# Layer norms of a two-block transformer kernel: centred on the mean of the first half of the tiles, with their sums inside the product ahead

## The chip, the cores and the metric

The kernel runs on one core of a Trainium2 chip. The time is device microseconds from the first to the last instruction's work of one launch; lower is better. Engines are named as in the profile: PE is TensorE (PEld its weight loads), DVE VectorE, ACT ScalarE, SP the queue that issues the DMAs.

## What is computed

Two blocks of two layers each on 256 tokens of width 2048, all in float32. The change concerns the first block:

```python
for layer in range(2):
    y = mixer(x) @ w_out                          # layer 0: rwkv7 + rglru, layer 1: sparse attention
    x = layer_norm(ALPHA * x + y, ln1_g, ln1_b)
    x = layer_norm(ALPHA * x + conv_ffn(x), ln2_g, ln2_b)
    x = x + sigmoid(x @ ple_w_gate) * (p[layer] @ ple_w_proj)

def layer_norm(x, g, b, eps=1e-5):
    mu = mean(x); var = mean((x - mu) ** 2)
    return (x - mu) * rsqrt(var + eps) * g + b
```

The second block (RMS norms, three attentions, gates) follows and is not changed.

## The kernel before

**Layout.** Activations lie as 16 tiles of 128 features by 256 tokens (`xav`, `xbv`), so that a mean over features is a sum over partitions and tiles: a matmul with a 128x128 matrix of ones (`m("ones")`), one per tile, gives it, repeated on all partitions. `res` is the buffer that takes ALPHA * x + y, `x` the input; after the norm `x` holds the result.

**A product.** Weights come in pieces of 2 MB (1.4 MB for `down`) into a ring of three slots. Each piece has two halves of 128 output features. ACT rounds a half to fp32r (`split`, high part, semaphore `w_hi`), DVE subtracts to get the low part (`w_lo`), and PE does three groups of matmuls: high weights on the high and on the low part of the activations, low weights on the high part. There is one buffer per half, so ACT can write it only when PE has done with it. A unit is two halves into one PSUM bank, or, for the `up` products, into a bank per half; three banks take turns (`bank_free`), five more take the small jobs (`open_job`, `done`). A `down` unit has four pieces. The activations are split in the same way, in four parts of four tiles (`rhs`; `r_hi` from ACT, `r_lo` from DVE).

**A norm.** There are four: `ln0` after `ev_out`, `ln1` after `down0`, `ln2` after `od_out`, `ln3` after `down1`. `residual` evicts each unit on DVE. When all are out, `layer_norm` runs on three engines: PE sums 16 tiles (L783), DVE centres them (L1881) and ACT squares them (L1440), PE sums the squares (L802), then variance, square root, reciprocal, and for each part scaling on DVE, gain and bias on two tiles by each engine, and the split. The next product, `up` or `pg`, takes high parts first, then low parts. After `ln1` and `ln3` PE also does the embedding product `pp` (eight units of four f32 matmuls, L767), which DVE evicts behind the norm (L2386).

**Order.** Every engine's order is the order of the code. Products with many units are hardware loops over three units (`rounds`, L342) where no `after` function is given: `ev_out`, `od_out`, `down0`, `down1`, `pg0` and the `up` products among them.

**The first mixer's input product** `ea`, `eb`, `ec` goes by weight halves p = 0 to 42, with the mixer's element work beside them, keyed to p on each engine. At p = 29 PE sums the squares of `kk` (L852), at p = 33 it spreads their reciprocal roots (L861); at p = 42 DVE makes `KM`, on which the semaphore `elem` stands.

## Time and profile before

| | |
|---|---|
| median of 3 runs | 3715.66 us (3715.22 to 3721.29) |
| profiled execution, its own time | 3714.28 us |
| its span | 3712.5 us |
| PE busy | 3494.2 us (94%) |
| DVE busy | 2196.9 us (59%) |
| ACT busy | 1691.6 us (46%) |
| DMA, mean over the span | 152 GB/s |
| mean granted clock of PE | 0.970 |

The granted clock is a share of 2.4 GHz; the other level is 1.2 GHz, 0.50. In a timeline row the first two numbers are the start and the length in us, and the bracket at its end is the idle time of the engine ahead of it and who ended it; f32 matmuls have two records per instruction.

### The profile page before, as it was taken

What the parts mean: (1) busy time and instruction counts of PE and PEld (TensorE: products, weight loads), DVE (VectorE), ACT (ScalarE), POOL (GpSimd) and SP (SyncE); (2) the same over time, 40 slices, a digit from 0 to 9 for tenths busy, and PEclk for the clock granted to TensorE, in tenths of its full rate; (3) what the DMA queues carried; (4) which work ended last, traced back from release to release, by engine and by line L of the source; (5) the groups of instructions that cost most, each with busy time, mean ns of one, the idle gap of its engine ahead of it and who ended that gap; (6) DMA issues with size and microseconds to landing.
All of it is one profiled execution on the core that took longest, in us unless ns stands there. A gap on an engine that the chain in (4) does not pass through costs nothing.

```text
span 3712.5 us, 56634 instructions
## 1 busy us (share of the span) xinstructions
PE 3494.2 (94%) x23204; PEld 3196.2 (86%) x23204; DVE 2196.9 (59%) x2674; ACT 1691.6 (46%) x2030; POOL 0.2 (0%) x4
## 2 busy tenths in 40 slices
PE   8988969999998998988989999989989999899988
PEld 7878969788888997977988888889989888898878
DVE  5485764666666345535456666654456568456674
ACT  4562223565556333423345566553344455344553
POOL 0000000000000000000000000000000000000000
PEclk9999979999999999999999999999999999999999
DMA  6440025355553443531334454444524434444332
GB/s 254 159 159 24 2 91 181 127 190 181 186 198 131 165 181 134 188 150 55 123 126 182 183 195 187 167 152 177 209 114 172 173 134 148 157 150 183 135 140 110
DMA packets 45084, 563.78 MB, mean 152 GB/s; under 512 B 4832, under 2 KB 7024, under 8 KB 8048
## 3 DMA queue, kind: packets, MB, share of 16 engines
q1 hardware_dynamic: 44912, 561.27, 40.9%
q8 instruction: 134, 2.20, 0.2%
q14 instruction: 38, 0.31, 0.0%
HBM read 559.13 MB, written 2.12 MB: 151 GB/s over the span
## 4 chain that ended last, share of the span: by engine, by line
PE 85%; DVE 7%; ACT 4%; issue 3%; DMA 1%; DVEq 0%; ACTq 0%; SPq 0%
PE bank L707 28%; PE bank L711 15%; PE bank L657 5%; PE bank L653 5%; PE bank L648 5%; PE bank L748 4%; PE bank L751 4%; PE bank L756 4%; PE bank L783 4%; PE bank L767 2%; DVE ring L1875 1%; ACT spl_r L1365 1%; DVE scr L1881 1%; PE bank L802 1%; PE bank L954 1%
## 5 line engine op out<-in xcount | busy, mean ns | idle before, releaser
L1875 DVE TENSOR_TENSOR spl_r<-ring,spl_r 128x2048 fp32r<-128x2048 f32 x415 | 950.1, 2291 | 657.5 <-ACT spl_r L1365 656.2
L707 PE MATMUL bank<-all_r,spl_r 128*128 128x512 f32 x5008 | 1212.2, 394 | 1.6 <-ACT spl_r L1365 1.6
L1365 ACT ACTIVATE spl_r<-ring 128x2048 fp32r<-128x2048 f32 x415 | 793.1, 1912 | 759.9 <-PE bank L711 400.4
L707 PEld LDWEIGHTS bank<-all_r,spl_r 128*128 128x128 f32 x5008 | 924.7, 189 | 192.3 <-issue 7.9
L711 PEld LDWEIGHTS bank<-all_r,spl_r 128*128 128x128 f32 x5104 | 654.6, 191 | 24.4
L711 PE MATMUL bank<-all_r,spl_r 128*128 128x256 f32 x5104 | 662.4, 283 | 0.0
L1875 DVE TENSOR_TENSOR dsp_r<-ring,dsp_r 128x1408 fp32r<-128x1408 f32 x128 | 207.3, 1625 | 290.4 <-ACT dsp_r L1365 290.4
L1365 ACT ACTIVATE dsp_r<-ring 128x1408 fp32r<-128x1408 f32 x128 | 175.6, 1377 | 297.3 <-PE bank L756 297.2
L1881 DVE SCALAR_TENSOR_TENSOR scr<-sumbuf,vec,scr 128x255 f32<-128x255 f32 (+1 forms) x379 | 183.0, 483 | 118.0 <-ACT scr L1458 80.7
L648 PE MATMUL bank<-scr_r,spl_r 128*128 128x256 f32 x1536 | 209.6, 290 | 37.6 <-ACT scr_r L1319 35.8
L648 PEld LDWEIGHTS bank<-scr_r,spl_r 128*128 128x128 f32 x1536 | 196.2, 195 | 41.3 <-ACT scr_r L1319 33.5
L748 PE MATMUL bank<-scr_r,dsp_r 128*128 128x256 f32 x1408 | 195.3, 288 | 26.6 <-ACT dsp_r L1365 22.2
L748 PEld LDWEIGHTS bank<-scr_r,dsp_r 128*128 128x128 f32 x1408 | 182.2, 196 | 27.3 <-ACT dsp_r L1365 23.8
L653 PE MATMUL bank<-scr_r,spl_r 128*128 128x256 f32 x1536 | 204.2, 287 | 0.0
L657 PE MATMUL bank<-scr_r,spl_r 128*128 128x256 f32 x1536 | 201.1, 284 | 1.3 <-DVE spl_r L1875 1.3
L653 PEld LDWEIGHTS bank<-scr_r,spl_r 128*128 128x128 f32 x1536 | 195.7, 196 | 0.0
L657 PEld LDWEIGHTS bank<-scr_r,spl_r 128*128 128x128 f32 x1536 | 192.3, 193 | 1.8 <-DVE spl_r L1875 1.8
L751 PE MATMUL bank<-lo_r,dsp_r 128*128 128x256 f32 x1408 | 193.3, 286 | 0.0
L756 PE MATMUL bank<-scr_r,dsp_r 128*128 128x256 f32 x1408 | 190.8, 284 | 0.0
L1458 ACT ACTIVATE scr<-sumbuf,vec 128x256 f32<-128x256 f32 x176 | 105.3, 598 | 187.6 <-DVE sumbuf L1875 187.4
L751 PEld LDWEIGHTS bank<-lo_r,dsp_r 128*128 128x128 f32 x1408 | 182.0, 196 | 1.2 <-issue 1.2
L756 PEld LDWEIGHTS bank<-scr_r,dsp_r 128*128 128x128 f32 x1408 | 179.2, 193 | 0.0
(335 smaller groups left out, 2972.3 us busy)
## 6 DMA issues: line engine op xcount, KB each, us to landing
ring<-in_up SPq DMA_DIRECT2D x88, 2048.0 KB, 8.0
ring<-in_down SPq DMA_DIRECT2D x64, 1408.0 KB, 6.0
ring<-in_ib SPq DMA_DIRECT2D x34, 2048.0 KB, 8.2
ring<-in_pg SPq DMA_DIRECT2D x16, 2048.0 KB, 8.1
ring<-in_out SPq DMA_DIRECT2D x16, 2048.0 KB, 7.8
ring<-in_in SPq DMA_DIRECT2D x12, 2048.0 KB, 7.9
ring<-in_ec SPq DMA_DIRECT2D x11, 2048.0 KB, 9.1
ring<-in_ea SPq DMA_DIRECT2D x9, 2048.0 KB, 8.3
```

What stands on the lines that cost most here:

```text
L648: mm(out_, WHI[half][:, kk, :], rhi[:, kk, :], start=i_ == 0, stop=False)
L653: mm(out_, WHI[half][:, kk, :], rlo[:, kk, :], start=False, stop=False)
L657: one = mm(out_, WLO[half][:, kk, :], rhi[:, kk, :], start=False, stop=kk == DT - 1)
L707: mm(b[:, :], WHI[half][:, kk, :], pair(name, kk), start=kk == 0, stop=False, skip_group_check=True)
L711: one = mm(main, WLO[half][:, kk, :], rhi[:, kk, :], start=False, stop=kk == DT - 1, skip_group_check=True)
L748: mm(out_, DHI[half][:, kk, :], HHI[:, piece * FC + kk, :], start=first and kk == 0, stop=False, skip_group_check=True)
L751: mm(out_, DHI[half][:, kk, :], HLO[:, low_slot(piece * FC + kk), :], start=False, stop=False, skip_group_check=True)
L756: one = mm(out_, DLO[half][:, kk, :], HHI[:, piece * FC + kk, :], start=False, stop=last and kk == FC - 1, skip_group_check=True)
L783: one = mm(out, lhsT, rhs, start=n == 0, stop=n == len(terms) - 1)
L1365: A(high[half], w[:, :, half * P:(half + 1) * P], ACT.Copy).then_inc(S["w_hi"], count)
L1875: return V.tensor_tensor(out, a, b, op)
L1881: return V.scalar_tensor_tensor(out=out, in0=a, scalar=s, in1=b, op0=op0, op1=op1)
```

## The change

`residual` and `layer_norm` become one function per engine, `normed` (DVE, ACT) and `norm_sums` (PE), called after every unit of the product, which is written out unit by unit.

- While units 1 to 3 come out, DVE adds the first eight tiles up pairwise into two tiles of `x`; behind unit 4 PE sums these two, and DVE subtracts this mean of the first half (`SV`) from the ten tiles that are out. Units 5 to 7 are centred on it in their eviction (`x` is scaled and lowered ahead of it).
- ACT squares as tiles come; DVE adds squares up to four tiles. PE sums tiles 8 to 15 (whose mean gives what is still missing) and the squares, 4 matmuls behind unit 6 and 10 behind unit 7.
- Behind that: variance as mean of squares less the square of the mean, square root with the bias eps on ACT, reciprocal, and per part recentring and scaling on DVE, gain and bias on all four tiles and the high part on ACT.
- The next product's unit 0 (`both_halves`) takes the activations part by part, for both weight halves.
- The embedding product's unit 0 goes ahead of the last sums, its other units behind them, and ACT evicts them. Its input is loaded behind the `up` weights, into another place.
- In the first mixer the `kk` sum goes from p = 29 to 30, the spreading from 33 to 35, and `KM` behind the loop over p.

```diff
@@ SP
             def embedding(l):
-                sp.wait_ge(S["g_done"], STEP0[f"pp{l}"])
+                sp.wait_ge(S["g_done"], STEP0[f"up{l}"] + 2)
                 sp.dma_start(PIN, dram["p"][l]).then_inc(S["in_p"], 16)
...
                 stream(f"up{l}", FT)
+                embedding(l)
                 stream(f"down{l}", 32)
                 load(f"pp{l}", 0)
-                stream(f"pg{l}", 8, (2, lambda: embedding(l)))
+                stream(f"pg{l}", 8)
@@ PE
+            def both_halves(name, high, low, units):
...
+                def from_high(part):
+                    pe.wait_ge(S["r_hi"], 4 * n + part + 1)
+                    for half, w in ((0, WHI[0]), (0, WLO[0]), (1, WHI[1])):
+                        for kk in range(4 * part, 4 * part + 4):
+                            fresh = kk == 0 and w is not WLO[0] and (half == 0 or len(units) == 2)
+                            mm(high[half], w[:, kk, :], rhi[:, kk, :], start=fresh, stop=False, skip_group_check=True)
...
+                from_high(0)
+                from_high(1)
+                from_high(2)
+                from_low(0)
+                from_high(3)
+                for part in range(1, 4):
+                    from_low(part)
+                pe.wait_ge(S["w_lo"], first + 2)
+                for kk in range(DT):
+                    one = mm(high[1], WLO[1][:, kk, :], rhi[:, kk, :], start=False, stop=kk == DT - 1,
+                             skip_group_check=True)
+                one.then_inc(S["g_done"], 1)
...
-                rounds(pe, UNITS[name][0], unit)
+                for k in range(UNITS[name][0]):
+                    unit(k, 0)
+                    after(k)
...
+            def norm_sums(n, name, x, res, k):
+                mean, var = (f"ln{n}_mean", 0), (f"ln{n}_var", 0)
+                if k == 4:
+                    b = open_job(mean)
+                    pe.wait_ge(S["ln_sum"], n + 1)
+                    done(acc(b[:, 0:T], [(m("ones"), x[:, i, :]) for i in range(2)]))
+                if k == 6:
+                    b = open_job(var)
+                    pe.wait_ge(S["ln_cent"], 3 * n + 3)
+                    pe.wait_ge(*free_of(name, 5))
+                    for i in range(8, 12):
+                        mm(b[:, T:2 * T], m("ones"), res[:, i, :], start=i == 8, stop=False, skip_group_check=True)
+                if k == 7:
+                    b = job_bank(JOB[var])
+                    pe.wait_ge(S["ln_add"], n + 1)
+                    for i in range(4):
+                        mm(b[:, 0:T], m("ones"), x[:, i, :], start=False, stop=False, skip_group_check=True)
+                    pe.wait_ge(*free_of(name, 6))
+                    for i in range(12, 16):
+                        if i == 14:
+                            pe.wait_ge(*free_of(name, 7))
+                        mm(b[:, T:2 * T], m("ones"), res[:, i, :], start=False, stop=i == 15, skip_group_check=True)
+                    pe.wait_ge(S["ln_sq"], 6 * n + 6)
+                    for i in range(14, 16):
+                        one = mm(b[:, 0:T], m("ones"), x[:, i, :], start=False, stop=i == 15, skip_group_check=True)
+                    done(one)
...
+                def after(k):
+                    if k == 7:
+                        pe.wait_ge(S["in_p"], 16 * (l + 1))
+                        arrived(f"pp{l}")
+                        embedded(0)
+                    norm_sums(2 * l + 1, f"down{l}", x, res, k)
+
+                down(f"down{l}", after)
+                for k in range(1, 8):
+                    embedded(k)
...
-                if p == 29:
+                if p == 30:
...
-                if p == 33:
+                if p == 35:
@@ ACT, def normed(name, n, x, res)
+                for k in range(8):
+                    if k < 7:
+                        ahead(k, 0)
+                    if k == 5:
+                        for part in range(3):
+                            act.wait_ge(S["ln_cent"], 3 * n + part + 1)
+                            square(4 * part, min(4 * part + 4, 10))
+                    if k >= 6:
+                        act.wait_ge(*free_of(name, k - 1))
+                        square(2 * k - 2, 2 * k)
+                    if k < 7:
+                        ahead(k, 1)
+                    elif not down_:
+                        split(nxt, 0, 0, 1, (0,))
+                act.wait_ge(*free_of(name, 7))
+                square(14, 16)
+                if down_:
+                    embedded(0)
+                act.wait_ge(S["ln_var"], n + 1)
+                A(RV, RV, ACT.Sqrt, bias=v("eps")).then_inc(S["ln_std"], 1)
+                if down_:
+                    embedded(1)
+                    split(nxt, 0, 0, 1, (0,))
+                    embedded(2)
+                    split(nxt, 0, 0, 1, (1,))
+                    embedded(3)
+                else:
+                    split(nxt, 0, 0, 1, (1,))
                 for part in range(4):
...
+                    high(part)
+                    if down_:
+                        embedded(4 + part)
@@ DVE, def normed(name, n, x, res)
+                def evict(k):
+                    u = UNIT0[name] + k
+                    pair_ = slice(2 * k, 2 * k + 2)
+                    if k > 4:
+                        link(stt(x[:, pair_, :], x[:, pair_, :], ALPHA, repeat(SV, 2), ALU.mult, ALU.subtract))
+                    unit_wait(name, k, 0)
...
+                for k in range(8):
+                    if k < 7:
+                        ahead(k, 0)
+                    else:
+                        ve.wait_ge(S["ln_sq"], 6 * n + 5)
+                        linked(add_squares(12, 2), S["ln_add"], n + 1)
+                        if not down_:
+                            split(nxt, 0, 0, 1, (0,))
+                    evict(k)
...
+                    if k == 4:
+                        key = (f"ln{n}_mean", 0)
+                        b = job_wait(key)
+                        linked(ts(SV, b[:, 0:T], 2.0 / D), job_free(JOB[key]), freed(JOB[key]))
+                        ve.wait_ge(*free_of(name, 4))
+                        for first, last in ((0, 4), (4, 8), (8, 10)):
+                            tt(res[:, first:last, :], res[:, first:last, :], repeat(SV, last - first), ALU.subtract)\
+                                .then_inc(S["ln_cent"], 1)
...
+                    if k < 7:
+                        ahead(k, 1)
...
+                cent(0)
+                ve.wait_ge(S["ln_std"], n + 1)
+                link(V.reciprocal(RV, RV))
+                scaled(0)
+                for part in range(1, 4):
+                    if down_ and part > 1:
+                        split(nxt, 0, 0, 1, (part - 2,))
+                    cent(part)
+                    scaled(part)
+                    if not down_ and part > 1:
+                        rhs(nxt, part - 2, part - 1)
...
-                if p == 42:
-                    tt(KM, ZK, CUM, ALU.mult).then_inc(S["elem"], 1)
+            tt(KM, ZK, CUM, ALU.mult).then_inc(S["elem"], 1)
```

**TensorE at the end of `ev_out` and the start of `up0`, before.** `bank` is a PSUM bank, `xa` and `xb` the activation buffers, `mat` holds the ones.

```order
L653 MATMUL bank<-scr_r,spl_r 128x256 x16
L657 MATMUL bank<-scr_r,spl_r 128x256 x16
L783 MATMUL bank<-xb,mat 128x256 x16
L802 MATMUL bank<-xa,mat 128x256 x16
L698 MATMUL bank<-all_r,spl_r 128x256 x16
L703 MATMUL bank<-all_r,spl_r 128x256 x16
L711 MATMUL bank<-all_r,spl_r 128x256 x16
L707 MATMUL bank<-all_r,spl_r 128x512 x16
L711 MATMUL bank<-all_r,spl_r 128x256 x16
```

The same place after the change:

```order
L662 MATMUL bank<-scr_r,spl_r 128x256 x16
L666 MATMUL bank<-scr_r,spl_r 128x256 x16
L868 MATMUL bank<-xa,mat 128x256 x4
L873 MATMUL bank<-xb,mat 128x256 x4
L876 MATMUL bank<-xa,mat 128x256 x2
L742 MATMUL bank<-all_r,spl_r 128x256 x36
L748 MATMUL bank<-all_r,spl_r 128x256 x8
L742 MATMUL bank<-all_r,spl_r 128x256 x12
L748 MATMUL bank<-all_r,spl_r 128x256 x24
L762 MATMUL bank<-all_r,spl_r 128x256 x16
```

The 32 matmuls on ones behind the last product matmul are now ten (six more stand in the product, two behind unit 4, four behind unit 6), and unit 0 of `up0` comes in groups by part.

**ScalarE from the last `down0` weights to the high parts for `pg0`, before.** `dsp_r` and `spl_r` are rounded weights, `scr_r` the high part of the activations, `rstd` and later `xtra` the row of variances.

```order
L1365 ACTIVATE dsp_r<-ring 128x1408 x8
L1365 ACTIVATE spl_r<-ring 128x2048 x2
L1440 ACTIVATE xa<-xb 128x1024 x4
L1443 ACT_TABLE_LOAD
L1443 ACTIVATE rstd<-rstd 128x256
L1314 ACTIVATE xa<-xa,vec 128x256 x2
L1319 ACTIVATE scr_r<-xa 128x1024
L1314 ACTIVATE xa<-xa,vec 128x256 x2
L1319 ACTIVATE scr_r<-xa 128x1024
L1314 ACTIVATE xa<-xa,vec 128x256 x2
```

The same place after the change:

```order
L1435 ACTIVATE dsp_r<-ring 128x1408 x6
L1513 ACTIVATE xa<-xb 128x512 x2
L1518 ACTIVATE scr<-bank 128x512
L1549 ACT_TABLE_LOAD
L1549 ACTIVATE xtra<-xtra,vec 128x256
L1518 ACTIVATE scr<-bank 128x512
L1435 ACTIVATE spl_r<-ring 128x2048
L1518 ACTIVATE scr<-bank 128x512
L1435 ACTIVATE spl_r<-ring 128x2048
L1518 ACTIVATE scr<-bank 128x512
L1524 ACTIVATE xa<-xa,vec 128x256 x4
L1528 ACTIVATE scr_r<-xa 128x1024
```

The weight halves of `pg0` moved behind the square root, between copies of embedding units out of PSUM, of which three stand ahead of the first part and one behind each part; gain and bias go over four tiles instead of two.

**VectorE in the product `ev_out`, before,** in the last turn outside the loop:

```order
L1881 SCALAR_TENSOR_TENSOR xb<-xa,bank 128x512
L342 REGISTER_ALU
L342 COMPARE_AND_BRANCH
L1875 TENSOR_TENSOR spl_r<-ring,spl_r 128x2048 x2
L1881 SCALAR_TENSOR_TENSOR xb<-xa,bank 128x512 x2
```

After the change, around unit 4:

```order
L1986 TENSOR_TENSOR spl_r<-ring,spl_r 128x2048 x2
L1992 SCALAR_TENSOR_TENSOR xb<-xa,bank 128x512
L1989 TENSOR_SCALAR xtra<-bank 128x256
L1986 TENSOR_TENSOR xb<-xb,xtra 128x1024 x2
L1986 TENSOR_TENSOR xb<-xb,xtra 128x512
L1986 TENSOR_TENSOR spl_r<-ring,spl_r 128x2048 x2
L1992 SCALAR_TENSOR_TENSOR xa<-xa,xtra 128x512
L1986 TENSOR_TENSOR xb<-xa,bank 128x512
```

The mean of the first half and three centrings stand between the eviction of unit 4 and the low part of the next weight half.

## Rows read from the trace of the kernel before

**Rows 1.** The page's part 4: share of the chain that ended last, by engine.
```profile
PE 85%; DVE 7%; ACT 4%; issue 3%; DMA 1%; DVEq 0%; ACTq 0%; SPq 0%
```

**Rows 2.** Windows: start:end, length, busy us of each engine, granted clock, DMA share, GB/s.
```profile
634.00:677.00 43.00, 30.46 (x146) 26.43 (x145) 26.71 (x27) 18.40 (x21) 0.00 (x0) 0.84 0.14 50
1436.00:1491.00 55.00, 41.27 (x224) 36.86 (x225) 31.51 (x34) 19.68 (x21) 0.00 (x0) 0.91 0.23 91
1894.00:1938.00 44.00, 31.45 (x148) 26.92 (x148) 26.71 (x27) 19.58 (x22) 0.00 (x0) 0.81 0.13 48
2689.00:2744.00 55.00, 41.42 (x226) 37.01 (x227) 31.36 (x34) 19.54 (x21) 0.00 (x0) 0.91 0.23 91
```

**Rows 3.** Timeline of PE, first norm: start, us, engine, line, operation [idle before].
```profile
630.29 2.08 PE L653 MATMUL bank<-scr_r,spl_r 128*128 128x256 f32 x16
632.21 2.08 PE L657 MATMUL bank<-scr_r,spl_r 128*128 128x256 f32 x16
...
644.96 7.15 PE L802 MATMUL bank<-xa,mat 128*128 128x256 f32 x32 [2.50 <-ACT xa L1440]
658.49 1.19 PE L698 MATMUL bank<-all_r,spl_r 128*128 128x256 f32 x4 [6.38 <-ACT all_r L1319]
...
665.81 3.62 PE L703 MATMUL bank<-all_r,spl_r 128*128 128x256 f32 x16
...
675.29 2.08 PE L711 MATMUL bank<-all_r,spl_r 128*128 128x256 f32 x16
```

**Rows 4.** Timeline of PE, norm after down0, to unit 1 of pg0.
```profile
1434.28 1.48 PE L756 MATMUL bank<-scr_r,dsp_r 128*128 128x256 f32 x11
...
1453.42 5.34 PE L767 MATMUL bank<-scr,ring 128*128 128x256 f32 x24
...
1491.07 2.08 PE L648 MATMUL bank<-scr_r,spl_r 128*128 128x256 f32 x16
```

**Rows 5.** Timeline of DVE, end of ev_out and first norm.
```profile
613.24 2.29 DVE L1875 TENSOR_TENSOR spl_r<-ring,spl_r 128x2048 fp32r<-128x2048 f32 x1 [3.47 <-ACT spl_r L1365]
...
634.40 0.69 DVE L1881 SCALAR_TENSOR_TENSOR xb<-xa,bank 128x512 f32<-128x512 f32 x1 [6.75 <-PE bank L657]
...
653.05 1.75 DVE L2343 RECIPROCAL rstd<-rstd 128x256 f32<-128x256 f32 x1 [0.48 <-ACT rstd L1443]
654.84 1.23 DVE L1875 TENSOR_TENSOR xa<-xb,rstd 128x1024 f32<-128x1024 f32 x1
```

**Rows 6.** Timeline of ACT, first norm and up0; last row: pg0's first gate.
```profile
656.10 1.09 ACT L1314 ACTIVATE xa<-xa,vec 128x256 f32<-128x256 f32 x2 [3.08 <-DVE xa L1875]
657.28 1.06 ACT L1319 ACTIVATE all_r<-xa 128x1024 fp32r<-128x1024 f32 x1
...
671.84 1.91 ACT L1365 ACTIVATE spl_r<-ring 128x2048 fp32r<-128x2048 f32 x1 [5.80 <-PE bank L711]
...
1494.49 0.60 ACT L1481 ACTIVATE scr<-bank 128x512 f32<-128x512 f32 x1
```

**Rows 7.** Window in the first norm, columns as in the windows above.
```profile
662.00:666.00 4.00, 2.43 (x9) 2.14 (x10) 4.00 (x6) 3.89 (x5) 0.00 (x0) 0.50 0.00 0
```

**Rows 8.** Timeline of PE in the first mixer's input product and behind it.
```profile
209.80 1.94 PE L852 MATMUL bank<-scr,mat 128*32 128x256 f32 x16 [4.52 <-ACT scr L1581]
...
239.96 2.11 PE L861 MATMUL bank<-sumbuf,mat 32*128 32x256 f32 x16 [5.14 <-DVE sumbuf L2084]
...
297.27 2.73 PE L869 MATMUL bank<-mat,scr 128*128 128x128 f32 x16 [4.10 <-DVE scr L1881]
```

**Rows 9.** Window over the second half of the product ec.
```profile
211.58:297.21 85.63, 76.45 (x436) 66.44 (x432) 78.20 (x72) 45.47 (x61) 0.00 (x0) 0.95 0.31 111
```

**Rows 10.** Timeline of PE at the turn of down0's loop.
```profile
1273.39 1.61 PE L748 MATMUL bank<-scr_r,dsp_r 128*128 128x256 f32 x10 [3.23 <-issue]
1276.16 0.37 PE L748 MATMUL bank<-scr_r,dsp_r 128*128 128x256 f32 x1 [1.16 <-issue]
```

**Rows 11.** Window over the eight written-out units of pg1.
```profile
2744.00:2833.00 89.00, 88.16 (x714) 87.21 (x713) 48.70 (x44) 42.55 (x47) 0.00 (x0) 1.00 0.45 166
```

More of the change, by code:

```diff
@@ L509, in build, with free_of @@
             n_low += 2 * UNITS[name][0]
+        LN_NEXT = ("up0", "pg0", "up1", "pg1")
+        def free_of(name, k):
+            u = UNIT0[name] + k
+            return bank_free[u % R3], 2 * (u // R3) + 4
         def freed_unit(name, k, half, i):
@@ L1067, in _ @@
             group_norm_var(1)
-            product("ev_out")
-            layer_norm(0, xbv)
+            product("ev_out", after=lambda k: norm_sums(0, "ev_out", xav, xbv, k))
             ffn(0, xav, xbv)
@@ L1684, in _ @@
             rhs("ev_out", 2)
[L1685 to L1687 removed]
+            normed("ev_out", 0, xav, xbv)
             ffn(0, xav)
@@ L2324, in residual @@
-                for un in range(UNIT0[name] + 5, UNIT0[name] + 8):
-                    ve.wait_ge(bank_free[un % R3], 2 * (un // R3) + 4)
-                ve.engine_nop().then_inc(S["resid"] if scale != 1.0 else S["x_ready"],
-                                                            8 if scale != 1.0 else 1)
-            def layer_norm(n, res, dst, gain, bias, col):
-                split(("up0", "pg0", "up1", "pg1")[n], 0, 0)
-                b = job_wait((f"ln{n}_mean", 0))
-                for part in range(4):
-                    sl = slice(4 * part, 4 * part + 4)
-                    stt(res[:, sl, :], repeat(b[:, 0:T], 4), -1.0 / D, res[:, sl, :]).then_inc(S["ln_cent"], 1)
-                ve.wait_ge(S["ln_cent"], 4 * n + 4)
-                ve.engine_nop().then_inc(job_free(JOB[(f"ln{n}_mean", 0)]), 1)
+                else:
+                    rhs(name)
+                    split(name, 0, 0)
@@ L2343, in layer_norm @@
-                link(V.reciprocal(rstd[:, 0:T], rstd[:, 0:T]))
-                for part in range(4):
-                    sl = slice(4 * part, 4 * part + 4)
-                    linked(tt(dst[:, sl, :], res[:, sl, :], repeat(rstd[:, 0:T], 4), ALU.mult),
-                           S["ln_y"], 4 * n + part + 1)
-                    for i in range(4 * part, 4 * part + 2):
-                        one = ts(dst[:, i, :], dst[:, i, :], v(gain, col + i), v(bias, col + i), ALU.mult, ALU.add)
-                    one.then_inc(S["x_part"], 1)
@@ L2353, in layer_norm, with cent, scaled @@
-                rhs(("up0", "pg0", "up1", "pg1")[n])
+                def cent(part):
+                    sl = slice(4 * part, 4 * part + 4)
+                    link(tt(res[:, sl, :], res[:, sl, :], repeat(SV, 4), ALU.subtract))
+                def scaled(part):
+                    sl = slice(4 * part, 4 * part + 4)
+                    tt(x[:, sl, :], res[:, sl, :], repeat(RV, 4), ALU.mult).then_inc(S["ln_y"], 1)
+                cent(0)
+                ve.wait_ge(S["ln_std"], n + 1)
+                link(V.reciprocal(RV, RV))
```

190 lines of the change are left out of this document (107 added, 83 removed).

## The prediction

> **What bounds the kernel now.** I read the chain that ended last first: TensorE has 85% of it [rows 1], so time is won only where TensorE waits, or works on something that can go. The windows over the four layer norms come next [rows 2]. In the two after `ev_out` and `od_out` TensorE is busy for 30.46 of 43 us and 31.45 of 44 us; in the two after the `down` products for 41.27 and 41.42 of 55 us, and much of that is the sums of the norm and the embedding product. The reader is to see that a norm costs TensorE far more than its idle time, so I measure each norm from the last product matmul (T) to the end of the next product's unit 0.
>
> After `ev_out`, T is 632.21 + 2.08 = 634.3 us; the sums of squares end at 652.1, the first `up0` matmul starts at 658.49, and unit 0 ends when the pair of rows from 675.29 ends, at 677.2 [rows 3]: **42.9 us**. After `od_out` the same rows repeat (two norms of this kind) and the window is one us longer; by the same two matmuls it is **43.6 us**. After `down0` T is 1435.8, the embedding product starts at 1453.42 and unit 1 of `pg0` starts at 1491.07 [rows 4]: **55.3 us**. After `down1` the window [rows 2] has the same length and busy time; I take 55.2.
>
> **What the new sequence takes behind T.** Prices: a `ones` matmul on one f32 tile takes 7.15/16 = 0.45 us [rows 3], an embedding unit of four such tiles 5.34/3 = 1.8 [rows 4]. A product matmul takes, in steady pace 0.12 us (groups of 16 start 1.92 apart), and 3.62/16 = 0.226 at the low clock [rows 3]. VectorE: eviction of a unit 0.69, reciprocal 1.75, four tiles by a repeated row 1.23, low half of a weight half 2.29 [rows 5]. ScalarE: two gained tiles 1.09, copy of four tiles 1.06, high half of a weight half 1.91, a unit out of PSUM 0.60 [rows 6].
>
> After `ev_out`/`od_out`, in us behind T: the last eviction (0.8) and the last two squares on ScalarE (a pair of tiles, 0.60 by the nearest row [rows 6], to 1.5) lie beside ten `ones` matmuls, 10 x 0.45 = 4.5. Three small VectorE steps are not in this form in the trace; they are half as wide as an eviction (0.69), so between 0.35 and 0.7 each; with handing on I take 1.7 in all: 6.2. Recentring part 0 (1.23), reciprocal (1.75), scaling (1.23): 10.5. ScalarE's square root and its high half of weight half 1 lie beside these. Now ScalarE sets the pace: four gained tiles and a copy, 2 x 1.09 + 1.06 = 3.2 per part, where VectorE needs 2 x 1.23. Parts are ready at 13.8, 17.0, 20.2 and 23.4. TensorE works on each as it comes; behind the last stand 12 matmuls, 24 on low parts and 16 on the low weights of half 1, 52 x 0.12 = 6.2, and I add 2 for the clock and for the third part, on which 20 matmuls stand: **31.6**.
>
> The clock was at 0.50 from 662 to 666 us [rows 7], the lower level of 1.2 GHz, behind a pause of six us and short bursts. It was back before 675.29, where 16 matmuls take 2.08, and what came before that was unbroken matmuls from 665.81 on [rows 3]. After the change TensorE pauses about 9 us, and its bursts (12 matmuls, 2.7 us at that level, in every 3.2) are nearly unbroken, and quite so from part 2 on. So I let the clock be low for parts 0 to 2 and full for what stands behind part 3; if it came back only behind unit 0, the 52 matmuls would take 11.8 us instead of 6.2, rival (a).
>
> In-product costs: two `ones` matmuls behind unit 4 and four behind unit 6 go into TensorE's row, 6 x 0.45 = **2.7** per norm. VectorE gets up to 5.2 us more in unit 4 (0.69, a wait for the mean of 2 x 0.45, its copy of 0.4, three centrings of ten tiles, 3.1) between the two weight halves. Its low half then ends 7.5 us behind the unit's end, and TensorE wants it at 5.76 + 3.84 = 9.6: two us to spare, so nothing. In units 5 and 6 it is 0.69 + 0.69 + 1.23. VectorE works 5.3 of every 11.5 us there now (two of 2.29 and one of 0.69 [rows 5]); were that cover gone, up to 3 us per unit would show. In the `down` products a unit lasts 31.7 us and nothing shows.
>
> Gain there: 42.9 - 31.6 - 2.7 = 8.6 and 43.6 - 34.3 = 9.3.
>
> After the `down` products: an embedding unit (1.8) goes ahead of the ten `ones` matmuls: 6.3, row work to 8.0, square root 8.4. ScalarE then has three units out of PSUM (0.60) and two weight halves (1.91): 5.6, so 14.0 (at 8.4 + 5.6); this, not VectorE's scaling at 12.3, is last. Four parts of 3.2 with three copies of 0.60 between them: 14.0 + 12.9 + 1.8 = 28.7. The embedding's last unit waits for the PSUM bank that ScalarE empties behind part 0, about 17.9, and ends at 19.7; TensorE starts on parts 0 and 1 then and has done them when part 2 comes. Behind part 3: 6.2, plus 1.3 for pauses: **36.2**, with 2.7 in the product 38.9. Gain 16.4 and 16.3. That ScalarE empties the embedding's banks while TensorE has nothing else is most of this.
>
> Sum over the norms: 50.6.
>
> **The first mixer.** The sum for `kk` goes one weight half later, the product that spreads it two halves later. TensorE waited 4.52 and 5.14 us before them and then 4.10 before the transposes [rows 8]. These waits are not all to be had, for VectorE becomes last: from 211.58 to 297.21 us it is busy 78.20 of 85.63 us [rows 9], idle 7.4, and it can't begin earlier: its first step there is the low half of the next weights behind ScalarE's high half, and that stands behind the squares of `kk` which the first of the three waits names [rows 8]. `KM` (eight tiles, 2.3 by the row for four [rows 5]) goes behind the last shift, off the transposes' path. Upper bound 7.4 + 2.3 = 9.7, lower 3: following VectorE's steps with its splits I get 3.0 at once, some 2 of the small waits, and 2.3 from `KM`: **7.4**, near the upper row.
>
> **Loops written out.** `ev_out`, `od_out`, `down0`, `down1` and `pg0` were loops on three engines. In `down0` TensorE waited 3.23 + 1.16 us for "issue" at the turn of the loop [rows 10], and 33 matmuls behind it ran low, about 2.3 us more: **6.7**. `down1` shows no such gap, so between 0 (it comes at some other place) and 7.5; written-out stretches show none, as `pg1` with TensorE busy 88.16 of 89 us [rows 11]. I take 6.7, what `down0` shows. The Trainium skill (Runtime: NRT & Kernel Launch, "Instruction fetch mechanics") says that a taken branch whose target lies outside the part held in instruction memory stalls for a fetch, while straight code is fetched ahead. By it both `down` loops, with 1584 matmul and weight-load instructions in a turn, would have paid, 13.4 in all; the trace has one gap, 6.7.
>
> The embedding's input goes earlier in the SP queue, ahead of `down`'s weights; 0.26 MB among 2 MB loads, hidden behind the ring's three slots: 0.
>
> **Sum.** 50.6 + 7.4 + 6.7 = 64.7, less 2 for handings between engines that I have not counted = 62.7. From the profiled execution's 3714.28: 3651.6; it lies 1.4 under the median shown. I say **3652**.
>
> **Rivals.**
> (a) Low clock through unit 0 at each norm: 5 us more each, 3672. For it: the pause is longer than now. Against: TensorE is then busy 2.7 of every 3.2 us. 0.10.
> (b) The written-out code keeps the gap elsewhere and the first mixer gives only 3: 3652 + 6.7 + 4.4 = 3663. For it: `down1` had none without the change. 0.15.
> (c) VectorE's centring makes the weights' low halves late in units 4 to 6: up to 5 us a norm, 3672. Against: two us to spare by the sum. 0.10.
> (d) Slower: the written-out `down` units each bring a fetch gap like the one at the loop's turn. At 6.7 each, over 9 such gaps eat the gain; one in each of 16 `down` units gives 3652 + 107 = 3759. Against: the written-out stretch that shows none [rows 11]. 0.03.
> (e) The norms' tails are as long as now because ScalarE's doubled share (3.2 against 2.15 per part) eats what the sums gave: it costs 4.3 per norm, already in; no change overall needs four times that. 0.03.
> Forecast: 0.59.
>
> **The numbers.** The forecast's own bounds: row steps, clock and mixer, 3640 to 3662. To leave out 2 in 10 the range reaches into (a) and (c): 3638 to 3674. A difference under 0.2% (7.4 us) can't be told from none. Faster 0.94, same 0.03, slower 0.03.
>
> **What would show it.** Per norm: T to the end of unit 0 near 32 and 36 us; part 0 about 14 behind T after `ev_out`; embedding units evicted by ScalarE; no TensorE wait in units 4 to 7; TensorE's waits at the two `kk` matmuls gone and small waits for VectorE's low halves in their place; no issue gap in `down0`. Wrong would be the sum if ScalarE's parts came slower than 3.2 us, or the ten `ones` matmuls waited for squares.

## The result and the profile after

| | before | after |
|---|---|---|
| median | 3716.29 us (3715.22 to 3721.29, 4 runs) | 3634.31 us (3632.09 to 3638.96, 4 runs) |
| profiled execution, its span | 3714.28, 3712.5 us | 3633.78, 3632.0 us |
| granted clock, mean | 0.970 | 0.976 |

The ratio is 0.9778 with a 95% interval of 0.9762 to 0.9795: 82 us faster by the medians, 80.5 us by the profiled executions. I had forecast 3652 (3638 to 3674), 62.7 us. The sign was right; the gain was underestimated by 17.8 us (80.5 less 62.7), and the median lies 3.7 us below the range.

The page of the changed kernel: the first line of part 1, and part 4 by engine, against [rows 1]:

```profile
PE 3452.0 (95%) x23108; PEld 3161.6 (87%) x23108; DVE 2221.1 (61%) x2686; ACT 1715.1 (47%) x2086; POOL 0.2 (0%) x4
...
PE 84%; DVE 7%; ACT 5%; issue 3%; DMA 1%; DVEq 0%; ACTq 0%; SPq 0%
```

TensorE has 42 us less busy time than before (3494.2) in a span 80.5 us shorter. ScalarE has one point more of the chain, the work it took over in the norms.

The windows over the four tails, each from T to the first matmul behind unit 0, against [rows 2]; columns as there:

```profile
624.45:653.37 28.92, 19.22 (x118) 17.66 (x117) 20.23 (x19) 18.60 (x26) 0.00 (x0) 0.82 0.19 73
1407.35:1440.59 33.24, 30.61 (x183) 27.41 (x182) 22.37 (x20) 24.01 (x34) 0.00 (x0) 1.00 0.37 150
1849.17:1878.11 28.94, 18.06 (x119) 16.52 (x118) 20.25 (x19) 19.90 (x27) 0.00 (x0) 0.88 0.20 72
2632.09:2665.33 33.24, 30.61 (x182) 27.41 (x181) 22.37 (x20) 24.02 (x34) 0.00 (x0) 1.00 0.38 152
```

A tail is the time from T, the end of the last product matmul, to the end of the next product's unit 0. The tails were 42.9, 55.3, 43.6 and 55.2 us. They are now 28.9, 33.2, 28.9 and 33.2. Behind the `down` products TensorE is busy 30.61 of 33.24 us, where it was 41.27 of 55: the embedding product now fills the wait.

**The first norm.** TensorE (the timeline, as in [rows 3]):

```profile
624.45 1.89 PE L868 MATMUL bank<-xa,mat 128*128 128x256 f32 x8
...
627.90 1.03 PE L876 MATMUL bank<-xa,mat 128*128 128x256 f32 x4
637.96 5.82 PE L742 MATMUL bank<-all_r,spl_r 128*128 128x256 f32 x24 [9.03 <-ACT all_r L1528]
643.98 1.70 PE L742 MATMUL bank<-all_r,spl_r 128*128 128x256 f32 x12 [0.20 <-ACT all_r L1528]
...
647.04 1.70 PE L742 MATMUL bank<-all_r,spl_r 128*128 128x256 f32 x12 [0.40 <-ACT all_r L1528]
...
651.45 2.08 PE L762 MATMUL bank<-all_r,spl_r 128*128 128x256 f32 x16
653.37 2.00 PE L720 MATMUL bank<-all_r,spl_r 128*128 128x512 f32 x8
```

VectorE's row work and first part, and ScalarE's parts, in the same stretch:

```profile
630.35 1.22 DVE L1986 TENSOR_TENSOR xb<-xb,xtra 128x1024 f32<-128x1024 f32 x1
...
633.39 1.22 DVE L1986 TENSOR_TENSOR xa<-xb,xtra 128x1024 f32<-128x1024 f32 x1
```

```profile
634.65 2.08 ACT L1524 ACTIVATE xa<-xa,vec 128x256 f32<-128x256 f32 x4 [2.00 <-DVE xa L1986]
636.76 1.06 ACT L1528 ACTIVATE all_r<-xa 128x1024 fp32r<-128x1024 f32 x1
637.72 2.06 ACT L1524 ACTIVATE xa<-xa,vec 128x256 f32<-128x256 f32 x4
```

Read from T = 624.45, the sums are done at 4.5 us, the variance at 5.9, the first scaled part at 10.2 and part 0 at 13.5. Before, the sums ended 17.8 us behind T and the first `up0` matmul began at 24.2 [rows 3]. A part then comes every 3.06 us (634.65 to 637.72 on ScalarE), so part 3 is there at 22.6 (647.04). What stands behind it ends at 28.9, which is 6.3 us for 52 matmuls at 0.12. The records of neighbouring rows overlap, so a part's pace is read from starts, not from the sum of lengths.

**The second norm**, TensorE, against [rows 4]:

```profile
1407.35 1.89 PE L825 MATMUL bank<-xtra,ring 128*128 128x256 f32 x8
...
1424.12 1.99 PE L825 MATMUL bank<-xtra,ring 128*128 128x256 f32 x8 [0.21 <-ACT scr L1518]
1427.66 4.76 PE L742 MATMUL bank<-scr_r,spl_r 128*128 128x256 f32 x36 [1.54 <-ACT scr L1518]
...
1434.26 1.69 PE L742 MATMUL bank<-scr_r,spl_r 128*128 128x256 f32 x12 [0.88 <-ACT scr_r L1528]
```

and before, the embedding's other units, whose wait [rows 4] does not show:

```profile
1469.23 10.50 PE L767 MATMUL bank<-scr,ring 128*128 128x256 f32 x40 [10.47 <-DVE scr L2386]
```

ScalarE empties the embedding's banks (`scr`, L1518), and TensorE waits 0.21, 1.54 and 0.88 us in the whole tail. Before, it waited 1.00 and 2.50 us at the sums, and 10.47 us for VectorE's eviction behind the embedding's third unit.

**The first mixer**, TensorE's waits, against [rows 8]:

```profile
207.16 1.07 PE L934 MATMUL bank<-scr,mat 128*32 128x256 f32 x16
...
238.10 2.17 PE L724 MATMUL bank<-all_r,spl_r 128*128 128x256 f32 x16 [2.37 <-DVE spl_r L1986]
240.20 1.17 PE L943 MATMUL bank<-sumbuf,mat 32*128 32x256 f32 x16
...
285.40 3.49 PE L951 MATMUL bank<-mat,scr 128*128 128x128 f32 x16 [4.34 <-DVE scr L1992]
```

The two waits at the `kk` matmuls (4.52 and 5.14 us) are gone. In their place stand three for VectorE's low halves, 1.08, 2.37 and 0.25 us. The wait before the transposes is still there, 4.34 us where it was 4.10: `KM` is out of VectorE's way, but TensorE arrives earlier. No wait of TensorE for "issue" is left in `down0`, nor one for anything in the units 4 to 7 of `ev_out`.

### The profile page after: what moved, and what is told of

Same layout as the page of the kernel before. It is cut to its first block, busy times and chain, and to the rows that moved or that the text cites. A ratio compares the mean times of both kernels' runs of the same rounds, so it can differ in the third digit from the quotient of the medians.

```text
span 3632.0 us, 56135 instructions
## 1 busy us (share of the span) xinstructions
PE 3452.0 (95%) x23108; PEld 3161.6 (87%) x23108; DVE 2221.1 (61%) x2686; ACT 1715.1 (47%) x2086; POOL 0.2 (0%) x4
## 3 DMA queue, kind: packets, MB, share of 16 engines
q8 instruction: 144, 2.36, 0.3%
## 4 chain that ended last, share of the span: by engine, by line
PE 84%; DVE 7%; ACT 5%; issue 3%; DMA 1%; DVEq 0%; ACTq 0%; SPq 0%
PE bank L720 28%; PE bank L724 15%; PE bank L666 5%; PE bank L662 5%; PE bank L657 5%; PE bank L804 4%; PE bank L807 4%; PE bank L812 4%; PE bank L841 3%; PE bank L825 2%; ACT spl_r L1435 1%; DVE ring L1986 1%; DVE scr L1992 1%; PE bank L1036 1%; DVE scr L1986 1%
## 5 line engine op out<-in xcount | busy, mean ns | idle before, releaser
L720 PEld LDWEIGHTS bank<-all_r,spl_r 128*128 128x128 f32 x4976 | 917.0, 188 | 189.4 <-issue 6.8
L724 PEld LDWEIGHTS bank<-all_r,spl_r 128*128 128x128 f32 x5040 | 645.7, 191 | 29.0 <-DVE spl_r L1986 5.0
L724 PE MATMUL bank<-all_r,spl_r 128*128 128x256 f32 x5040 | 653.9, 283 | 3.7 <-DVE spl_r L1986 3.7
L657 PE MATMUL bank<-scr_r,spl_r 128*128 128x256 f32 x1472 | 201.3, 290 | 37.9 <-ACT scr_r L1389 36.1
L657 PEld LDWEIGHTS bank<-scr_r,spl_r 128*128 128x128 f32 x1472 | 188.1, 194 | 41.9 <-ACT scr_r L1389 33.8
L662 PE MATMUL bank<-scr_r,spl_r 128*128 128x256 f32 x1472 | 194.6, 286 | 0.0
L666 PE MATMUL bank<-scr_r,spl_r 128*128 128x256 f32 x1472 | 191.8, 283 | 1.6 <-DVE spl_r L1986 1.6
L662 PEld LDWEIGHTS bank<-scr_r,spl_r 128*128 128x128 f32 x1472 | 186.6, 195 | 0.0
L666 PEld LDWEIGHTS bank<-scr_r,spl_r 128*128 128x128 f32 x1472 | 183.2, 192 | 2.0 <-DVE spl_r L1986 2.0
```

Source lines behind the costliest of these rows:

```text
L657: mm(out_, WHI[half][:, kk, :], rhi[:, kk, :], start=i_ == 0, stop=False)
L662: mm(out_, WHI[half][:, kk, :], rlo[:, kk, :], start=False, stop=False)
L666: one = mm(out_, WLO[half][:, kk, :], rhi[:, kk, :], start=False, stop=kk == DT - 1)
L720: mm(b[:, :], WHI[half][:, kk, :], pair(name, kk), start=kk == 0, stop=False, skip_group_check=True)
L724: one = mm(main, WLO[half][:, kk, :], rhi[:, kk, :], start=False, stop=kk == DT - 1, skip_group_check=True)
```

## Experiments

Each kernel has 4 to 11 runs. The kernel before has its own runs in each group, so a ratio compares on the same chip. The times are medians. The changed kernel itself was run twice more, as the level for its variants; the group of **embed_behind**, **old_unit0**, **no_adds** and **two_gains** has no run of it, and is set against 3633 from the other two (the kernel before has 3716.9 in that group, 3716.8 and 3715.6 in those).

> The changed kernel itself, beside the three others on the same chip. All theories: 80 to 84 us faster than before. With mixer_only and loops_only at 8 and 7, the norms alone would be worth about 66 us where 50.6 was forecast.

Measured 3632.86 us (3628.31 to 3635.3), ratio 0.9779 (0.9766 to 0.9793), 82 us faster as expected.

> The changed kernel itself beside the two others on the same chip, for a comparison with them of a few us: 3632 to 3636.

Measured 3633.4 us (3632.25 to 3634.12), ratio 0.9781 (0.9767 to 0.9794). The result stands, and 3633 is the level below.

### Parts of the change put alone into the kernel before

**km_only**: `KM` behind the last half.

```diff
-                if p == 42:
-                    tt(KM, ZK, CUM, ALU.mult).then_inc(S["elem"], 1)
+            tt(KM, ZK, CUM, ALU.mult).then_inc(S["elem"], 1)
```

> The kernel before with `KM` alone moved behind the loop over p. Theory A (the last shift is what the transposes wait for, and a 2.3 us instruction stands ahead of it): 2.3 us faster, the transposes' wait on TensorE 4.1 -> about 1.8 us. Theory B (the transposes wait for the weights' last unit, KM is only pushed onto the path behind them): no change, since `elem` comes at the same time and the first pair matmuls wait for it.

Measured 3713.37 us against 3716.82; ratio 0.9994 (0.9985 to 1.0003). The time alone doesn't tell A from B. The trace does: TensorE waits 2.17 us before the transposes instead of 4.10 [rows 8], and from its half at p = 29 to the transposes it takes 95.65 us instead of 97.64.

```profile
292.49 1.97 PE L869 MATMUL bank<-mat,scr 128*128 128x128 f32 x16 [2.17 <-DVE scr L1881]
```

**mixer_only**: that, and the two `kk` matmuls at p = 30 and 35.

```diff
-                if p == 29:
+                if p == 30:
...
-                if p == 33:
+                if p == 35:
```

> The kernel before with the three moves in the first mixer (kk sum to p = 30, spreading to p = 35, KM behind the loop), norms and loops as before. Theory A (VectorE is last once TensorE's two waits are gone): 7.4 to 8.5 us faster, small waits of TensorE for VectorE's low halves appear. Theory B (the mixer carries the surplus of the whole change over its forecast, as the 11.9 us between the two traces at the transposes suggest): 11 us or more.

Measured 3706.43 us; ratio 0.9975 (0.9965 to 0.9985), which is 9.3 us by the ratio and 10.4 by the medians. The interval, 5.6 to 13.0 us, holds both theories. The traces tell them apart. Windows from the start of TensorE's half at p = 29 to the transposes, with the same 482 matmul records in each, before and here; columns as in [rows 2]:

```profile
199.56:297.20 97.64, 83.95 (x482) 71.91 (x480) 86.14 (x80) 56.27 (x75) 0.00 (x0) 0.95 0.33 119
```

```profile
196.36:285.80 89.44, 82.66 (x482) 71.30 (x480) 83.73 (x80) 56.86 (x75) 0.00 (x0) 0.98 0.36 130
```

The stretch is 8.2 us shorter, as A has it. Of the 11.9 us by which the changed kernel is ahead of the kernel before at the transposes, 3.6 were there before p = 29, where nothing was changed. The waits for low halves are 1.10 and 2.36 us here too. The loop in `down0` is as before, and its gap is still there:

```profile
1263.14 2.41 PE L748 MATMUL bank<-scr_r,dsp_r 128*128 128x256 f32 x10 [3.16 <-issue]
```

**loops_only**: the products written out, in the order they had.

```diff
-                rounds(pe, UNITS[name][0], unit)
+                for k in range(UNITS[name][0]):
+                    unit(k, 0)
...
-                    rounds(ve, n - 1, body)
-                    body(n - 1, 0)
+                    for k in range(n):
+                        body(k, 0)
...
```

> The kernel before with `ev_out`, `od_out`, `down0`, `down1` and `pg0` written out on all three engines, nothing else changed. Theory A (one gap at the turn of down0's loop and the low clock behind it): 6.7 to 7.5 us faster, no issue gap in down0. Theory B (loop turns cost at every product): 13 us or more. Theory C (the fetch gap comes at some other place): 0.

Measured 3708.87 us; ratio 0.9977 (0.9968 to 0.9986), 8.5 us by the ratio (5.2 to 11.9) and 8.0 by the medians; that excludes theories B and C. TensorE's waits in `down0` by releaser (us in total, times, longest), first the kernel before, then this one:

```profile
PE bank L748 <- issue: 4.4, 2, 3.2
PE bank L748 <- ACT dsp_r L1365: 2.9, 2, 2.6
```

```profile
PE bank L748 <- ACT dsp_r L1366: 3.2, 3, 2.4
```

From its first matmul to T, `down0` lasts 260.4 us here (1165.25 to 1425.64) and 267.9 before, 7.5 us more. In **km_only** and **mixer_only**, which have the loop too, it lasts 265.8 and 265.7 with gaps of 3.44 and 3.16 + 0.37 us, so the gap costs 5.3 to 7.5 us. `down1`, where no gap shows, lasts 260.5 as a loop. What is left of the 8.5 lies inside the interval.

### Parts of the change undone

**embed_behind**: the embedding product behind the norm's sums and evicted by VectorE, as before; all else as changed. The lines below are TensorE's part; ScalarE's `embedded` calls are gone too, and VectorE copies the eight units behind `normed`.

```diff
                 def after(k):
                     if k == 7:
-                        pe.wait_ge(S["in_p"], 16 * (l + 1))
-                        arrived(f"pp{l}")
-                        embedded(0)
+                        pass
                     norm_sums(2 * l + 1, f"down{l}", x, res, k)
 
                 down(f"down{l}", after)
-                for k in range(1, 8):
+                pe.wait_ge(S["in_p"], 16 * (l + 1))
+                arrived(f"pp{l}")
+                for k in range(8):
                     embedded(k)
```

> The changed kernel with the embedding product as it was: all eight units behind the last sums and evicted by VectorE behind the norm (the input's early load stays). Theory A (the embedding's place beside the norm, with ScalarE emptying the banks, is what makes the two norms behind `down` gain 22 us instead of 14): slower than the changed kernel by 2 x 14 to 2 x 19, 3662 to 3672. Theory B (the gain of these norms comes from the sums and unit 0; TensorE would have waited for ScalarE's parts anyway): at most 10 us slower, 3644.

Measured 3665.28 us (3664.46 to 3666.57), 32 above the changed kernel. T is 1407.14:

```profile
1411.45 5.34 PE L825 MATMUL bank<-xtra,ring 128*128 128x256 f32 x24
1434.10 10.98 PE L825 MATMUL bank<-xtra,ring 128*128 128x256 f32 x40 [17.30 <-DVE scr L2542]
...
1456.42 2.08 PE L657 MATMUL bank<-scr_r,spl_r 128*128 128x256 f32 x16
```

Three units fill the three banks, and the fourth waits 17.30 us for VectorE. The tails are 49.3 and 49.6 instead of 33.2, 32.4 us more in all: A holds. The product's place and the engine that evicts it go back together here, so the run prices the two as one, 40% of the change's gain.

**old_unit0**: the next product's first unit all high parts first, then all low ones.

```diff
-                        if k == 0 and name[:2] == "pg":
+                        if False:
...
-                    if first and name[:2] == "up":
+                    if False:
```

> The changed kernel with the next product's unit 0 in the old order: 16 matmuls on high parts, 16 on low parts, 16 on low weights for half 0, then half 1. Behind the last part there are then 4 + 16 + 16 + 48 (44 us-equivalents of 0.12 for the wide form) matmuls instead of 52. Theory A (what stands behind the last part decides): 3.3 to 4 us per norm, 13 to 16 us slower, 3648 to 3650. Theory B (the weights' low halves or VectorE's low parts hold unit 0 anyway): 4 us or less.

Measured 3650.83 us (3648.58 to 3655.06), 17 above. T is 626.45:

```profile
639.96 1.19 PE L711 MATMUL bank<-all_r,spl_r 128*128 128x256 f32 x4 [9.03 <-ACT all_r L1528]
642.92 1.22 PE L711 MATMUL bank<-all_r,spl_r 128*128 128x256 f32 x4 [1.77 <-ACT all_r L1528]
...
650.05 3.62 PE L716 MATMUL bank<-all_r,spl_r 128*128 128x256 f32 x16
...
661.45 2.91 PE L720 MATMUL bank<-all_r,spl_r 128*128 128x512 f32 x12
```

The tail is 35.0 instead of 28.9, though part 0 comes at the same 13.5. Part 3 is there at T + 22.6 in both (its rows repeat the second one here, the last from 649.03). Of unit 0's 96 matmuls (a 128x512 one counted as two) the old order can do 12 before that, since only the first half's high group runs on parts alone; 84 stand behind it. In quarters it is 44 before and 52 behind. The 32 more take 3.8 us at 0.12. The rest, 2.3, is the clock: it is still at 0.50 behind the last part, so that 16 matmuls take 3.62 us there.

The four tails are 6.1, 5.7, 5.3 and 5.6 us longer, 22.7 in all, in a profiled execution of 3655.06 us, the slowest of the five. The median is 17 above the changed kernel's. Theory A holds in kind, but it had 3.3 to 4 us a norm, without the clock; why the medians show less than the tails is open.

**no_adds**: TensorE sums all 16 tiles of squares itself, VectorE adds none.

```diff
-                    for i in range(4):
+                    for i in range(14):
                         mm(b[:, 0:T], m("ones"), x[:, i, :], start=False, stop=False, skip_group_check=True)
...
-                        linked(add_squares(12, 2), S["ln_add"], n + 1)
+                        ve.engine_nop().then_inc(S["ln_add"], 1)
...
-                        link(add_squares(4, 4))
...
-                        link(add_squares(8, 4))
```

> The changed kernel, but VectorE doesn't add squares up; TensorE sums all 16 tiles of squares behind the product, 20 `ones` matmuls instead of 10. Theory A (TensorE's sums are the path from the last product matmul to the variance): 10 x 0.43 = 4.3 us per norm, 17 us slower, 3651. Theory B (ScalarE's work in between is last, at least behind the `down` products, where ScalarE has copies and weight halves ahead of the first part): 8.6 us from the other two norms only, 3643.

Measured 3650.55 us (3649.01 to 3650.82), 17 above, four times the ten matmuls of 0.43 us; each of the four tails is 4.3 us longer. A holds; nothing else was waiting in their place.

```profile
622.08 6.20 PE L868 MATMUL bank<-xa,mat 128*128 128x256 f32 x28
...
655.33 2.00 PE L720 MATMUL bank<-all_r,spl_r 128*128 128x512 f32 x8
```

### Suspected costs taken away

**warm**: 20 more `ones` matmuls in TensorE's pause of the norms behind `ev_out` and `od_out`.

```diff
+                if len(units) == 2:
+                    for _ in range(20):
+                        mm(high[0], m("ones"), m("mask", 256), start=True, stop=True, skip_group_check=True)
                 pe.wait_ge(S["w_lo"], first + 1)
```

> The changed kernel with 20 extra `ones` matmuls (8.6 us) into the next unit's bank in the pause of TensorE behind the norms after `ev_out` and `od_out`; they are overwritten. Theory A (the low clock behind the pause costs nothing, since the parts come at ScalarE's pace and the clock is back before part 3): within 1 us of the changed kernel. Theory B (the low clock costs, as the forecast had it with some 2 us per norm and as rival (a) had it with 5): 3 to 10 us faster.

Measured 3632.32 us (3628.45 to 3638.97), the changed kernel's level. T is 623.01:

```profile
627.33 8.80 PE L736 MATMUL bank<-mat 128*128 128x256 f32 x40
636.52 1.66 PE L745 MATMUL bank<-all_r,spl_r 128*128 128x256 f32 x12 [0.40 <-ACT all_r L1531]
639.49 1.69 PE L745 MATMUL bank<-all_r,spl_r 128*128 128x256 f32 x12 [1.31 <-ACT all_r L1531]
...
651.96 3.36 PE L720 MATMUL bank<-all_r,spl_r 128*128 128x512 f32 x14
```

The clock is full for part 0 (12 matmuls in 1.66 us), TensorE then waits 1.31 us for part 1 and as long for part 2, and the tail is 28.95 against 28.92. Behind `od_out` the tail is 28.95 too. So the low clock after the pause costs nothing where the parts come at ScalarE's pace. The median alone would not tell 1 us from 3.

**two_gains**: gain and bias on two of every four tiles; the kernel leaves them out on the other two, so it only shows what the work costs.

```diff
-                    for i in range(4 * part, 4 * part + 4):
+                    for i in range(4 * part, 4 * part + 2):
...
-                    act.wait_ge(S["x_act"], 16 * n + 4 * part + 4)
+                    act.wait_ge(S["x_act"], 8 * n + 2 * part + 2)
```

> The changed kernel with gain and bias left out on two of every four tiles (work left out, to relieve ScalarE by 1.03 us per part). Theory A (ScalarE sets the pace of the parts, 3.05 us, and VectorE's 2.3 to 3.4 us stand close behind it): 2 us per norm behind `ev_out` and `od_out`, where VectorE becomes last, and up to 4 behind `down`: 8 to 12 us faster, 3622 to 3626. Theory B (VectorE sets it): 2 us or less.

Measured 3628.67 us (3623.96 to 3632.55), 4.7 below 3633.4 and between A and B. ScalarE now waits for VectorE's scaled parts:

```profile
638.82 1.09 ACT L1524 ACTIVATE xa<-xa,vec 128x256 f32<-128x256 f32 x2 [0.21 <-DVE xa L1986]
...
644.75 1.09 ACT L1524 ACTIVATE xa<-xa,vec 128x256 f32<-128x256 f32 x2 [1.35 <-DVE xa L1986]
```

Behind `ev_out` the tail is 27.1 (T 626.23, unit 1 at 653.35), and behind `od_out` too; behind `down0` it is 33.45 and behind `down1` 32.1. So ScalarE sets the pace behind the mixers, though not by much: parts 1 and 2 each come 2.40 us behind the one ahead instead of 3.06, and part 3 comes 3.53 behind part 2, since VectorE's low part stands between. Behind `down` ScalarE does not set it alone.

**splits_ahead**: behind `down`, both halves of `pg`'s first weights are rounded ahead of the wait for the variance.

```diff
                     embedded(0)
+                    split(nxt, 0, 0, 1, (0,))
+                    split(nxt, 0, 0, 1, (1,))
                 act.wait_ge(S["ln_var"], n + 1)
...
                     embedded(1)
-                    split(nxt, 0, 0, 1, (0,))
                     embedded(2)
-                    split(nxt, 0, 0, 1, (1,))
```

> The changed kernel with both weight halves of `pg` rounded on ScalarE ahead of its wait for the variance instead of behind the square root. Theory A (behind the `down` norms ScalarE is last with its own queue: 5.6 us of copies and halves behind the square root, where VectorE's first part is ready 3.9 us behind it): part 0 starts 2 us earlier, 1.5 to 2 us per norm, 3 to 4 us faster than the changed kernel. Theory B (TensorE's embedding units, which wait for banks, are last): no change.

Measured 3632.55 us (3630.47 to 3636.55): no gain, so theory A's 3 to 4 us did not come. ScalarE begins its first part at T + 12.0 instead of T + 13.1, but VectorE (with its two low halves of 2.29 us between the parts) now ends last, and the tail is 33.1 (T 1410.70). Theory B is right in part: ScalarE also waits twice, 1.13 us each, for TensorE's embedding units ahead of its first part.

```profile
1435.37 1.21 PE L748 MATMUL bank<-scr_r,spl_r 128*128 128x256 f32 x8 [0.72 <-DVE scr_r L1986]
1437.44 1.70 PE L742 MATMUL bank<-scr_r,spl_r 128*128 128x256 f32 x12 [0.85 <-ACT scr_r L1528]
...
1443.78 2.08 PE L657 MATMUL bank<-scr_r,spl_r 128*128 128x256 f32 x16
```

**splits_both**: that, and VectorE takes its first low half ahead of the variance too.

```diff
+                if down_:
+                    split(nxt, 0, 0, 1, (0,))
                 key = (f"ln{n}_var", 0)
                 b = job_wait(key)
...
-                    if down_ and part > 1:
-                        split(nxt, 0, 0, 1, (part - 2,))
+                    if down_ and part > 2:
+                        split(nxt, 0, 0, 1, (1,))
```

> Both engines ahead in the norms behind down0 and down1: ScalarE rounds both halves of pg's weights ahead of the square root, as in the run before, and VectorE takes its low part of the first half ahead of the variance, where it waits 5.3 us, instead of between parts 1 and 2. Theory A (behind down ScalarE and VectorE are level, so only both together move the end): VectorE's last part comes about 1.8 us earlier, ScalarE's about 1.2 us; tails of 33.2 us become 32, and the time is 2 to 3 us below the changed kernel's, 3630 to 3632. Theory B (something else, such as the embedding units, sets the end): tails stay at 33.2 and the time at 3633.

Measured 3630.19 us (3628.53 to 3632.03), ratio 0.9766 (0.9752 to 0.9779).

```profile
1405.70 1.89 PE L825 MATMUL bank<-xtra,ring 128*128 128x256 f32 x8
...
1431.85 1.69 PE L742 MATMUL bank<-scr_r,spl_r 128*128 128x256 f32 x12 [0.89 <-ACT scr_r L1528]
...
1438.18 2.08 PE L657 MATMUL bank<-scr_r,spl_r 128*128 128x256 f32 x16
```

The tails are 32.5 and 32.5, 0.8 shorter, where A said 32. VectorE's wait is gone and ScalarE is last again. It is the lowest median of a kernel that does all the work, 3 us under the changed one, but the intervals overlap: the shorter tails are shown, a faster kernel is not.

## Why the prediction was off

**The step that failed is the size of "What the new sequence takes behind T"**, not its mechanism. Forecast 31.6 and 36.2 us, measured 28.9 and 33.2. That is 2.7 and 3.0 a norm, 11.3 over the four. The tails fell by 72.7 in all; less 2.6 in each product (below) the norms gave 62.3, where 50.6 was forecast.

- Behind T, row work and part 0 were near: part 0 forecast at 13.8, measured 13.5.
- "four gained tiles and a copy [...] 3.2 per part" was the sum of record lengths. The records overlap, and the pace from start to start is 3.06 us: part 3 came at 22.6 instead of 23.4. With the embedding's copies it is 3.54 a part, not 3.8, and the first begins at 13.1 instead of 14.0: part 3 came at 26.9 instead of 28.7. Together these are 2 x 0.8 + 2 x 1.8 = 5.2 us.
- "I add 2 for the clock and for the third part", and 1.3 behind `down`, were allowances without a row. Behind part 3 stand 6.3 us in both kinds. Behind `ev_out` the clock was indeed 0.50, but only on parts 0 and 1, at a time when TensorE would otherwise wait for ScalarE's next one, and **warm** shows that it costs nothing there; behind `down` it was 1.00 over the whole tail. This is the largest single piece, 2 x 1.9 + 2 x 1.2 = 6.2 us (6.3 measured less 6.2 forecast, each).

**First mixer**: 7.4 forecast, 8.2 in the traces of **mixer_only** up to the transposes (9.3 by its ratio, 5.6 to 13.0; bounds were 3 to 9.7). The mechanism is as forecast: the two waits vanish, small ones for VectorE's low halves come, and `KM` alone shortens the transposes' wait by 1.9. VectorE was last: from the `kk` sum to the transposes it is busy 75.62 of 77.24 us in the changed kernel.

**Loops written out**: 6.7 forecast, 8.5 by **loops_only** (5.2 to 11.9). The gap in `down0` cost 7.5 us in the kernel before and 5.3 and 5.4 in two others with the loop, so the forecast's 6.7 stands inside what the runs show. The Trainium skill (Runtime: NRT & Kernel Launch, "Instruction fetch mechanics") says that a taken branch stalls for a fetch when its target isn't in the current window of two pages (256 instructions each), and gives TensorE's instruction memory as 2048 instructions. A turn of the `down` loops has 1584: by the window both would have stalled, as the prediction reads it, and by the 2048 neither. The traces of three kernels with the loops show a gap in `down0` and none in `down1`, nor in `ev_out`, `od_out` and `pg0` (576 in a turn). So neither reading gives where it comes, and what decides it was not tried.

**"less 2 for handings between engines that I have not counted"**: no run shows such a term. In the tails the handings were already inside the rows' starts.

**The sum.** With the ratios of the two single runs it would be 62.3 + 9.3 + 8.5 = 80.1, against 80.5 between the profiled executions. That it closes so well is luck, since each ratio is uncertain by 3 to 4 us. The two traces themselves, by starts of rows, lay the 80.5 out so: 73.3 in the four tails (0.7 more than above, where T and the end of before were read from ends of records), 8.2 in the first mixer, 7.0 in `down0`, less 10.3 for the `ones` matmuls in the products; 3.6 lie before p = 29, where nothing was changed, and 2.0 behind the last changed unit; 3.3 were lost in other places, 2.8 of them between `pg0` and the end of `od_out`, for which I have no cause. So of the 17.8 us that I missed, the 11.7 of the norms are shown by the tails. The remaining 6 or so are of the size by which launches differ, and I can't share them out.

**In-product cost** of 2.7 a norm: the six `ones` matmuls take 0.43 each, 2.6, and no TensorE wait came with them in `ev_out` or `od_out`. Right.

**Rivals.** (a), low clock through unit 0: the clock was back with part 2. (b), gap elsewhere and the mixer at 3: both halves false. (c), low halves late in units 4 to 6: no wait there. (d), a fetch gap in each written-out `down` unit: none. (e), tails as long as now: they are 33% and 40% shorter. Every rival made the time longer. I had none in which my own allowances were too large, and so the range ended at 3638 where the time was 3634.

**Not tried by itself**: the mean of the first half. By the rows the sums end 4.5 us behind T instead of 17.8, the largest single shift behind the mixers, but no run puts it back alone.

## What to carry to other kernels

Take a pipelined engine's pace from the starts of successive instructions in the trace, not from the sum of their record lengths; with 3.06 and 3.54 a part for 3.2 and 3.8, this sum would have been some 3 us nearer. An allowance that no row asks for ("for the clock", "for handings") is a bias when all of them have the same sign: set it as a bound of the range, not as a term.

Where a product is there to fill a wait, look at which engine empties its PSUM banks, and choose one that is free at that moment. Putting the embedding's place and eviction back cost 32 us of 82, more than putting back the order in quarters (17) or leaving out VectorE's adding-up of squares (17). These parts were undone one at a time, so their prices need not add up.

## What the runs showed of the hardware

**The clock behind a pause, with two orders of the same work.** Windows of the changed kernel behind its 9 us pause, columns as in [rows 2]:

```profile
640.00:642.00 2.00, 1.94 (x10) 1.64 (x9) 1.97 (x3) 2.00 (x4) 0.00 (x0) 0.50 0.00 0
642.00:644.00 2.00, 1.80 (x10) 1.58 (x9) 2.00 (x3) 1.97 (x4) 0.00 (x0) 0.61 0.00 0
644.00:646.00 2.00, 2.00 (x16) 2.00 (x17) 2.00 (x2) 1.97 (x5) 0.00 (x0) 1.00 0.00 0
```

and of **old_unit0**, after a pause of the same length but with 4 matmuls where these have 12:

```profile
640.00:655.00 15.00, 9.56 (x41) 8.68 (x42) 10.48 (x9) 10.17 (x16) 0.00 (x0) 0.51 0.35 139
```

Between parts the one kernel has TensorE nearly without a gap and is at 2.4 GHz (1.00) some 6 us behind the pause; the other waits 1.8 us in every three and stays at 1.2 GHz (0.51 over these 15 us). The 6 us are no fixed size: behind `od_out`, with the same rows and the same pause of 9.03 us, the changed kernel has the full clock from 1866, 3.3 us behind its first matmul. I had let it be low for parts 0 to 2.

**The early part of a launch scatters.** The sum of `kk`'s squares, with the same wait of 4.52 us ahead of it and the same code up to there, starts at 209.80 us in the kernel before, 206.99 in km_only and 204.83 in loops_only. Single profiled executions can differ by 5 us before the change has had any effect, so terms of that size need the rounds, or a difference within one stage.
